# Two blocks of a layer on one core: where weight parts are made, and how three norms hand their tiles to the matrix engine

## What is computed

```python
def first_block(x, ...):
    h = rms_norm(x, pre_mix_norm)
    proj = h @ w_in                                   # attention and gated delta net inputs
    o_att = moba_attention(...); o_gdn = gated_deltanet(...)
    mix = concat([o_att, o_gdn]) @ w_out
    x = x + rms_norm(mix, post_mix_norm)
    h = rms_norm(x, pre_mlp_norm)
    m = square(relu(h @ w_up)) @ w_down
    x = x + rms_norm(m, post_mlp_norm)
    return x

def second_block(x, ...):
    h = rmsnorm(x, g_mix)                             # 'mix2' below
    ...                                               # convolution, retention, gates: merged
    x = x + merged @ w_o
    h2 = rmsnorm(x, g_ffn)                            # 'ffn' below
    x = x + (silu(h2 @ w_ff_gate) * (h2 @ w_ff_up)) @ w_ff_down
    return rmsnorm(x, g_final)
```

## Time and profile before

| | us |
|---|---|
| median of 3 timed runs | 956.87 (955.46 to 957.8) |
| profiled execution | 959.08, of which its span is 957.3 |
| PE busy | 924.0 |
| PE weight loads busy | 805.7 |
| DVE busy | 586.9 |
| ACT busy | 450.8 |
| POOL busy | 85.3 |

### The profile page before, as it was taken

One profiled execution on the slowest core, in us unless ns is written; L12 is line 12 of the kernel. 1 busy time (PEld: TensorE's weight loads), 2 busy tenths in 40 slices (PEclk: granted clock), 3 DMA queues, 4 the chain that ended last, 5 costly groups with the idle time before them and its releaser, 6 DMA issues.

```text
span 957.3 us, 12738 instructions
## 1 busy us (share of the span) xinstructions
PE 924.0 (97%) x5476; PEld 805.7 (84%) x5476; DVE 586.9 (61%) x668; ACT 450.8 (47%) x531; POOL 85.3 (9%) x92
## 2 busy tenths in 40 slices
PE   6999999979999999899999999999999899999997
PEld 5989878857888888799989988887888688888885
DVE  5689873567655566757764555545456646565554
ACT  5765365256444444645344234443443555444442
POOL 2033010010000000000031330101100000000000
PEclk9999999999999999999999999999999999999999
DMA  8634420324555445364573434453444444545441
GB/s 303 235 132 177 140 78 10 110 89 154 204 209 202 177 176 183 126 254 162 196 257 134 151 119 170 176 203 149 177 176 176 175 150 180 220 176 206 171 151 45
DMA packets 24217, 159.81 MB, mean 167 GB/s; under 512 B 3240, under 2 KB 3512, under 8 KB 5856
## 3 DMA queue, kind: packets, MB, share of 16 engines
q1 hardware_dynamic: 21600, 152.58, 43.3%
q0 software_dynamic: 2272, 6.24, 1.9%
q10 hardware_dynamic: 288, 0.17, 0.1%
HBM read 157.91 MB, written 2.63 MB: 168 GB/s over the span
## 4 chain that ended last, share of the span: by engine, by line
PE 85%; DVE 7%; ACT 5%; issue 2%; POOL 1%; DMA 0%; DVEq 0%; POOLq 0%; ACTq 0%
PE banks L478 30%; PE banks L420 22%; PE banks L446 14%; PE banks L449 7%; DVE t_wl L1430 2%; PE banks L503 2%; PE banks L399 2%; PE banks L946 1%; PE banks L561 1%; ACT t_wh L1014 1%; ACT t_hold L1022 1%; PE banks L719 1%; PE banks L742 1%; PE banks L897 1%; POOL t_st L1974 1%
## 5 line engine op out<-in xcount | busy, mean ns | idle before, releaser
L1430 DVE TENSOR_TENSOR t_wl<-t_raw,t_wh 128x2048 fp32r<-128x2048 f32 (+1 forms) x144 | 327.1, 2295 | 147.1 <-ACT t_wh L1014 145.5
L1014 ACT CAST t_wh<-t_raw 128x2048 fp32r<-128x2048 f32 (+1 forms) x144 | 268.8, 1900 | 31.7 <-PE banks L420 20.0
L420 PE MATMUL banks<-t_hx,t_wh 128*128 128x256 f32 x1232 | 225.8, 286 | 0.0
L420 PEld LDWEIGHTS banks<-t_hx,t_wh 128*128 128x128 f32 x1232 | 194.5, 194 | 2.3 <-DVE t_hx L1446 1.3
L446 PE MATMUL banks<-t_hx,t_wh 128*128 128x512 f32 x576 | 182.6, 399 | 2.1 <-DVE t_hx L1446 2.1
L420 PE MATMUL banks<-t_hx,t_wl 128*128 128x256 f32 x616 | 175.2, 284 | 0.0
L449 PEld LDWEIGHTS banks<-t_hx,t_wl 128*128 128x128 f32 x576 | 109.3, 190 | 25.8
L420 PEld LDWEIGHTS banks<-t_hx,t_wl 128*128 128x128 f32 x616 | 119.2, 194 | 0.0
L449 PE MATMUL banks<-t_hx,t_wl 128*128 128x256 f32 x576 | 114.0, 279 | 0.0
L478 PE MATMUL banks<-t_wh,t_hx 128*128 128x512 f32 x320 | 102.0, 395 | 0.0
L446 PEld LDWEIGHTS banks<-t_hx,t_wh 128*128 128x128 f32 x576 | 90.3, 191 | 4.1 <-DVE t_hx L1446 2.3
(11 more groups left out here) (291 smaller groups left out, 1217.8 us busy)
## 6 DMA issues: line engine op xcount, KB each, us to landing
t_raw<-in_W SPq DMA_DIRECT2D x143, 1024.0 KB, 4.9
skew<-scr POOLq DMA_DIRECT2D x1, 1536.0 KB, 17.4
t_x<-in_x SPq DMA_DIRECT2D x2, 512.0 KB, 4.9
t_T<-skew POOLq DMA_DIRECT2D x8, 128.0 KB, 2.4
out<-t_xt SPq DMA_DIRECT2D x4, 256.0 KB, 2.1
t_tab<-in_tab POOLq DMA_DIRECT2D x1, 640.0 KB, 6.2
t_raw<-in_W SPq DMA_DIRECT2D x1, 512.0 KB, 6.7
t_T<-skew POOLq DMA_DIRECT2D x8, 64.0 KB, 2.2
```

The costliest lines, as they stand in the source:

```text
L420: m = e.matmul(bank[b][:, c * S:c * S + S], W[w][:, h, k * 128 * nt + c * 128:k * 128 * nt + c * 128 + 128], H[a][:, k, :], start=first, s ...
L1014: e.copy(M.wh[:, h, 0:n], M.raw[:, r, 0:n]).then_inc(q.sem, q.tick(("hi", i)))
L1430: e.tensor_tensor(M.wl[:, h, 0:n], M.raw[:, r, 0:n], M.wh[:, h, 0:n].bitcast(F32), ALU.subtract).then_inc(q.sem, q.tick(("lo", i)))
```

## The change

It does five things.

1. Unit 17's parts are made one step earlier, within the last attention steps on ACT and DVE; the parts of units 18 and 19 take the places of 17 and 18; and unit 20 is made in two halves of 1024 columns (`hi_halves`, `lo_half`) beside the last `gated_norm`. Nothing of the weights stands between `turn_y(1)` and `between("mlp")` any more.
2. In `between`, the products and squares of the second tile are placed sooner: DVE does both products right behind the scaling of tile 0, ACT squares one half behind piece 1 and one behind piece 3, DVE's sum stands behind trailing part 4.
3. `place(k)` puts neighbouring pieces in two banks (0 and 2 in one, 1 and 3 in the next), DVE waits for one leading part only, and ACT waits for the trailing part of piece k-2 before it reads the other piece of that bank.
4. In the first MLP, DVE squares column block 0 ahead of unit 23, and PE's transposes for it come after the second k.
5. Before the gated MLP, tile 0 is transposed within the last product of `w_o` (ahead of its last six matmuls); gate unit 0 and up unit 0 are then multiplied for tile 0 with leading weights alone, tile 1 is transposed, and the rest follows. Both tiles' pieces are of 128 columns.

Helpers and PE:

```diff
+def place(k):
+    c = k % 4 // 2 * 128
+    return k // 4 * 2 + k % 2, slice(c, c + 128)
+def tiles_of(p):
+    k = p // 2 * 4 + p % 2
+    return k, k + 2
...
-                    if mid and k == 3:
+                    if mid and k == 1:
                         mid()
...
-            a_pair("wo", (M.gh, M.gl_), merged, (4, 5, 6, 7), acc)
...
-            turn_x("ffn")
+            def turn_first():
+                added_back(0)
+                turn_tile(0)
+            a_pair("wo", (M.gh, M.gl_), merged, (4, 5, 6, 7), acc, {(1, 18): turn_first})
+            added_back(1)
             q.mark("ffn")
+            pairs = [(tile, first[tile], next_unit()) for tile in ("fg", "fu")]
+            for t in range(2):
+                ts_ = slice(t * 128, t * 128 + 128)
+                for tile, b, i in pairs:
+                    ...
+                    for k in range(8):
+                        q.wait_ge(DV, ("xl", "ffn", t, k))
+                        for w in range(t + 1):
+                            for c in range(2):
+                                wk = slice(k * 256 + c * 128, k * 256 + c * 128 + 128)
+                                if w == 0:
+                                    e.matmul(halves(bank[b + c])[:, :, ts_], M.wh[:, h, wk], M.hx[:, k, :, ts_],
+                                             start=t == 0 and k == 0, stop=False, skip_group_check=True)
+                                else:
+                                    m = e.matmul(bank[b + c][:, 0:S], M.wl[:, h, wk], M.hh[:, k, :], start=False,
+                                                 stop=k == 7, skip_group_check=True)
+                    ...
+                if t == 0:
+                    turn_tile(1)
```

ACT:

```diff
+            def leading_of_x(g, t, k, w):
+                p, c = place(k)
+                q.wait_ge(PE, ("turn", g, t, p))
+                if k % 4 >= 2:
+                    q.wait_ge(DV, ("xl", g, t, k - 2))
+                e.activation(M.hh[:, k, t * 128:t * 128 + 128], bank[at["turn", g, t, p]][:, c], ACT.Copy,
+                             scale=w[:, k:k + 1]).then_inc(q.sem, q.tick(("xh", g, t, k)))
...
+                squares(0, 0)
+                squares(0, 1)
                 for t in range(2):
-                    for c in range(2):
-                        q.wait_ge(PE, (("mix" if g == "mlp" else "mlp"), t, c))
-                        square_of(bank[2 * t + c][:], M.part[:, 2 * t + c:2 * t + c + 1], ("psq", g, t, c))
                     norm_x(g, t)
                     scale_x(g, t)
                     for k in range(8):
+                        if t == 0 and k in (2, 4):
+                            squares(1, k // 2 - 1)
+                        leading_of_x(g, t, k, w)
...
             first_half(0)
+            att(2)
+            next_unit()
             att(len(STEPS) - taken[0])
...
             gated_norm(1, "o1")
             next_unit()
+            hi_halves()
+            next_unit()
             turn_y(1)
-            next_unit()
-            next_unit()
```

DVE:

```diff
                 ts(so, so, EPS, None, ALU.add, None, ("so1", c))
+                if c:
+                    lo_half(0)
                 q.wait_ge(PO, ("so", c))
...
             gated_norm(1)
+            lo_half(1)
             next_unit()
             turn_y(1)
-            next_unit()
-            next_unit()
...
+                    if t == 0:
+                        products(g, 1, arrived)
+                        trailing_of_x(g, 0, range(0, 5), w)
+                        mean_square(g, 1)
+                        trailing_of_x(g, 0, range(5, 8), w)
...
             for i in range(2, 16):
-                next_unit()
                 if i == 2:
                     square(0)
+                next_unit()
+                if i == 2:
                     square(1)
...
+            add_back("ffn", "wo", 1, lambda: trailing_of_x("ffn", 0, range(0, 4), w))
+            trailing_of_x("ffn", 0, range(4, 7), w)
+            norm_x("ffn", 1)
+            trailing_of_x("ffn", 0, range(7, 8), w)
+            scale_x("ffn", 1)
+            trailing_of_x("ffn", 1, range(8), w)
```

More of the change, by code:

```diff
@@ L979, in tensor, with turn_tile @@
             a_unit("A", ("wo", 1), (M.gh, M.gl_), merged, (2, 3), acc, False, False)
-            a_pair("wo", (M.gh, M.gl_), merged, (4, 5, 6, 7), acc)
-            for t in range(2):
+            first = {}
+            for tile in ("fg", "fu"):
+                turn[0] += turn[0] % 2
+                first[tile] = take((tile, 0))
+                take((tile, 0, 1))
+            def turn_tile(t):
+                for p, b in enumerate((0, 1, 2, 3) if t else (0, 1, first["fu"], first["fu"] + 1)):
+                    take(("turn", "ffn", t, p), b)
+                    opened(b)
+                    for k in tiles_of(p):
+                        q.wait_ge((DV, AC)[p // 2], ("xn", "ffn", t, p // 2))
+                        m = transpose(bank[b][:, place(k)[1]], M.xt[:, t, k * 128:k * 128 + 128])
+                    m.then_inc(q.sem, q.tick(("turn", "ffn", t, p)))
+                    drain(b, DV, ("xl", "ffn", t, tiles_of(p)[1]))
@@ L1018, in next_unit, with hi_halves @@
                 unit[0] += 1
+            def hi_halves():
+                i = done[0]
+                done[0] += 1
+                q.wait_dma(raw_in[i % RR], 16 * (i // RR + 1))
+                q.wait_ge(PE, ("unit", i - HR))
+                for p in range(2):
+                    e.copy(M.wh[:, i % HR, p * 1024:p * 1024 + 1024],
+                           M.raw[:, i % RR, p * 1024:p * 1024 + 1024]).then_inc(
+                               q.sem, q.tick(("hi", i, p), *[("hi", i)] * p))
             def square_of(a, o, name):
@@ L1381, in scalar @@
             next_unit()
-            for t in range(2):
-                norm_x("ffn", t)
-                scale_x("ffn", t)
-            turn_x("ffn", par("g_ffn"))
+            w = par("g_ffn")
+            norm_x("ffn", 0)
+            scale_x("ffn", 0)
+            for k in range(8):
+                if k in (4, 6):
+                    norm_half("ffn", 1, k // 2 - 2)
+                leading_of_x("ffn", 0, k, w)
+            scale_x("ffn", 1)
+            for k in range(8):
+                leading_of_x("ffn", 1, k, w)
             q.mark("ffn")
```

112 lines of the change are left out of this document (73 added, 39 removed).

## The result

| | median us | range | runs |
|---|---|---|---|
| before | 957.34 | 955.46 to 958.86 | 4 |
| after | 944.51 | 944.42 to 945.8 | 4 |

The ratio is 0.9869, 95% interval 0.9855 to 0.9882: 12.8 us faster. The forecast was 946.6, in a range of 944 to 950. The profiled execution of after took 944.42 with a span of 942.6, against 959.08 and 957.3.

What follows compares the result with a forecast made beforehand. PE was taken to lose time only standing still at joints or at a low clock behind them; 4.8 + 1.3 + 0.3 + 5.0 = 11.4 us, less 0.6 for the clock, gave 948.3 profiled, 946.6 timed, range 944 to 950.

Steps and rivals of the forecast that it cites:

- First joint: Before the first MLP: PE's 5.03 us wait goes; PE goes on at 217.8, waiting for unit 21, 4.8 us sooner.
- The clock: Behind tile 1's wait at the first joint: low clock half and half likely, at most 1.1 us, so 0.6 off.
- First MLP: At its first column block: the 1.3 us wait goes and nothing replaces it, since unit 23 is needed later.
- Second joint: Behind the first MLP: the 1.32 us gap ahead of tile 1 and low clock stay; 0.3 us gained, 1.4 if high.
- Third joint: Before the gated MLP: tile 0's early transposes and matmuls fill the waits, with about 1 us of holes; gain 5.0 us.
- The moved parts: Attention and gated norm: unit 17's cast fits an ACT hole, unit 20's half runs beside POOL's power; cost taken as 0.
- Rival A: Gated norm: DVE's half unit and POOL's power block each other, norm and PE 1.1 us later; 947.7, chance 0.17.
- Rival B: Third joint: small matmuls with short waits keep 1.2 GHz, PE ends first units 2.5 us later; 949.2, chance 0.13.
- C: Whole kernel: median shows nothing, norm's chain held by something counted free; 955 to 958, chance 0.04.
- D: All joints: slower, PE's stretches stay at 1.2 GHz until each joint's end; 962, chance 0.04.

Runs made afterwards that it cites:

- e5: The changed kernel with neighbouring pieces in one bank again and DVE waiting for a pair of leading parts: 944.48 us.
- e7: The changed kernel with both the sooner second-tile products and squares and the two-bank placement undone: 947.92 us.
- e2: The kernel before with only the weights' parts moved, nothing else: 952.58 us.
- e4: The kernel before with only the first MLP's new order (column block 0 ahead of unit 23, transposes two k sooner): 955.85 us.
- e3: The changed kernel with the old third joint (tile 0's early transposes and split first units undone): 949.47 us.
- e11: The changed kernel with dead DVE additions ahead of tile 1's scaling, two at the first joint, one at the second: 948.13 us.
- e8: The changed kernel with tile 1's squares and sum still sooner at the first two joints and the unit behind each made in halves: 944.08 us.
- e1: The changed kernel with the weights' parts behind turn_y(1) again, the rest of the change kept: 950.44 us.

## Why the prediction was right, and where it was short

In the order of its terms, forecast against the cuts:

- **First joint, 4.8 forecast, 5.56 measured.** The mechanism held in every step, on before's time axis (1.33 later): sum at 196.87 (196.95 forecast), ACT's first read at 202.14 (202.35), PE goes on at 217.26 waiting for unit 21 (217.8). Of the 0.76 us more, 0.22 is the place I counted from: the row at 222.60 is a weight load, and PE's first matmul of that unit is at 222.82. Another 0.21 is ACT's sooner first read. The last 0.33 is the path that ends in unit 21's part, 15.12 us behind that read where I had 15.45, because I did not carry tile 1's gain over to it. And tile 1's chain was mis-sized too: its matmuls start 8.96 us behind ACT's first read, I had 9.4. I held that the sooner sum would be lost behind three trailing parts. But `x`'s update starts 3.97 us behind that read instead of 4.32, and e5 against e7 prices part 2 by itself at 0.43 us. Part 3 takes 0.3 of it back, as I had counted for ACT's reads (2.61 us of 2.55 forecast); e2 shows that the two together are worth nothing at this joint.
- **The clock, 0.6 forecast as a loss at the first joint: nothing.** The wait ahead of tile 1 was 1.16 us, where no kernel's clock fell; my own times (208.1 and 210.3) made it 2.2 us, and behind 2.13 us and more it fell each time. So 947.2, the time with the first joint's tile 1 at the low clock, did not come.
- **First MLP, 1.3 forecast, 1.45 measured**, 1.56 alone (e4). Unit 23 was not missed.
- **Second joint, 0.3 forecast, 1.64 measured.** This is the step that failed: "This gap remains. Low again." Nearly all of it is the fall that did not happen, 1.58 us by e4, whose instructions at this joint are before's. The chain itself gave next to nothing: part 2 0.42 (16.06 in e4, 15.64 in e5), part 3 -0.36. I had the high clock at 1.4 us as the other bound, took the low one, and treated one trace's fall as a property of the code. What is not shown is why the clock stayed high in after: its wait was shorter too, 1.04 us instead of 1.32.
- **Third joint, 5.0 forecast, 4.8 measured** (5.0 by e3's median). I had 1 us of holes among tile 0's matmuls; one of 0.37 shows, but the 32 matmuls took 4.92 us from first to last, hole included, where I had counted 3.8 and 1: the sum is right, but 0.7 us of it lies inside the rows and not in a hole that the timeline lists. The first 12 took 1.96 us, 0.16 each; part of that is short waits, for at 750.6 to 750.9 PE was busy for 0.23 us and its weight loads for 0.01 of 0.30, while DVE made pieces of tile 0. Gate unit 1 was in time, 13.9 us behind w_o's end, where I had said at most 14. The 32 matmuls ran at 749.71 to 754.63 and not at 752 to 757, since the start and the first two joints had given more than forecast.

The sum is 13.4 against 10.8; the timed medians give 12.8. Without the fall's 1.58 the change gave 11.8 where the terms without the clock's 0.6 add up to 11.4, so the mechanism was right nearly to size. The time was off by 2.1 us, and the clock is the likeliest source: the 0.6 that I took off for it, and the falls that before pays and after does not. It fits that the kernel before pays for the second joint's fall in some executions only. The mean clock of its runs points the same way: of the 29 timed beside the experiments nine took 958.77 to 959.32 us at 0.991, like the profiled one (959.08, 0.991), and six 956.76 to 957.16 us at 0.994. A stretch of 3.4 us less at the low clock is worth 0.002 of that mean, but the mean does not say where a stretch lay, so in how many runs this joint fell is not shown.

The moved parts cost nothing, as forecast: from the first product of 16 columns to the mixer's end both kernels take 170.1 to 170.2 us, with unit 17's part in attention's last hole and the half units around the gated norm. Rival A did not come: POOL's power took 1.64 us beside DVE's half unit, as it did alone, and the half unit 1.23 us, as the other half did without POOL (1.22). So the rule of the Trainium skill, page "SBUF — State Buffer", section "🔬 SBUF: two separate sides", by which one of the two would have waited for the other's whole instruction, does not hold for this power, where the measurement decides. It may still be what makes POOL's 128 x 256 operations slow beside DVE in the earlier trace rows; what sets the two cases apart was not tried. Rival B did not come either, nor C or D: PEclk was 1.00 through all three joints.

## What to carry to other kernels

What stands in front of a norm's first sum, in the engines' queues, is worth its full length; what is placed sooner inside the chain behind it only its part that nothing else (here the next unit's cast) holds up. Cut the traces at the same places of the busiest engine's queue and add the stretches: a start that varies by 1.7 us and a clock that falls in one trace and not in another are then seen as what they are. A low clock in a single trace is a term with two values; look for a second execution with the same wait before carrying either as the kernel's own.

## What the runs showed of the hardware

- **The clock behind a wait of PE.** Ahead of tile 1's transposes, over both joints of thirteen kernels: behind waits of 2.13, 2.40 and 2.47 us it fell to 1.2 GHz each time; of seven waits between 1.32 and 1.63 us behind two (1.32 and 1.57, while other waits of 1.32, 1.33, 1.33, 1.56 and 1.63 had none); behind eleven waits of 0.57 to 1.16 us never. In e11 only the wait was changed. Each wait was seen in one execution, so the limits are those of these 21 waits and no more. A fall costs the 24 matmuls behind it 1.6 us (7.15 against 5.58 us at the second joint of before and of e4).
- **The start's spread is PE's pace.** The first 31 us took up to 1.7 us more or less in kernels that are the same there. 12 to 27 of PE's first matmuls of 256 columns ran at about half their later pace, and with their number went the time at which PE was through (30.48 us with 12 in e8, 31.87 with 27 in e1; e3, also with 12, began 0.26 us later than e8 and had 30.78). After alone began its first unit sooner, at 13.31 instead of 13.8 to 14.2 us, and had 16 slow ones (30.21).
- **Neighbouring pieces in two banks** let PE start 0.19 us behind its transposes (0.30 for tile 0 at the second joint) instead of 0.45, but make ACT's eight reads 2.6 us instead of 2.0. It pays where PE is next (third joint, 0.5 us) and costs where ACT is (0.3 us each).
